# Zeroing the expert sum rows in the window attention stage instead of the projection stage

## The reference

```python
mod = silu(cond) @ w_ada + b_ada                 # 6 x 1024 columns, for c_ctx and for c
h = modulate(rms_norm(x), shift1, scale1)
q_g, k_g, v_g, g_g, lora, q_s, k_s, v_s = split(h @ w_in)
gla  = gated_linear_attention(q_g, k_g, v_g, lora) -> rms_norm -> * silu(g_g)
attn = sink_softmax(q_s @ k_s) @ v_s             # tile 0: 128 context keys;
                                                 # latents: cached context keys + own tile and its neighbours
x = x + g1 * (concat(gla, attn) @ w_out)
x = x + g2 * moe(modulate(rms_norm(x), shift2, scale2))   # 64 experts, 8 per token, 1 shared
return rms_norm(x), new keys and values, new states
```

## Time and profile before

| | |
|---|---|
| median of 3 runs | 1649.61 us (1646.57 to 1650.51) |
| the profiled execution | 1649.61 us, span 1647.8 us |
| PE busy | 1510.6 us, 92% of the span |
| mean granted clock of TensorE | 0.956 of full |
| PE in window_attention (439.8 to 600.4 us) | busy 153.17 of 160.6 us |
| DMA | 297.40 MB in the whole run |

### The profile page before, as it was taken

How to read it: one execution, slowest core, us unless ns; L and a number is a source line. 1 busy time by engine, 2 the same in 40 slices (tenths; PEclk the granted TensorE clock), 3 DMA queues, 4 the chain that set the end, 5 groups by cost and what they waited for, 6 DMA issues and landing times. The chain is left out here.

```text
span 1647.8 us, 29332 instructions
## 1 busy us (share of the span) xinstructions
PE 1510.6 (92%) x9399; PEld 942.9 (57%) x9400; DVE 725.9 (44%) x1468; ACT 530.2 (32%) x1255; POOL 563.8 (34%) x615
## 2 busy tenths in 40 slices
PE   5999999999799999999999599999899999999745
PEld 2654678788677785555455355555455555555312
DVE  2300143442555563688752244444344444444238
ACT  2400174442265631121100133333333333333212
POOL 0001134343343211111145345555445555445422
PEclk7899999999899999999999799999999999999868
DMA  9981001100383032002000599999999999986487
GB/s 338 352 326 39 19 19 38 43 14 17 108 304 108 2 138 104 39 26 116 1 0 0 203 301 335 334 331 340 346 338 332 339 291 314 257 227 118 64 300 299
DMA packets 107962, 297.40 MB, mean 180 GB/s; under 512 B 12830, under 2 KB 23922, under 8 KB 107634
## 3 DMA queue, kind: packets, MB, share of 16 engines
q1 hardware_dynamic: 80674, 207.83, 33.4%
q0 software_dynamic: 25920, 83.91, 21.3%
q10 hardware_dynamic: 1296, 4.72, 0.7%
HBM read 226.02 MB, written 80.87 MB: 186 GB/s over the span
## 5 line engine op out<-in xcount | busy, mean ns | idle before, releaser
L2080 PE MATMUL ps_g<-w_exp,mix 128*64 x1408 | 327.1, 386 | 5.7 <-DVE own_gu L2175 2.8
L2083 PE MATMUL ps_g<-own_gu,mix 128*64 128x256 f32 x1408 | 327.1, 386 | 0.0
L2080 PEld LDWEIGHTS ps_g<-w_exp,mix 128*64 128x64 f32 x1408 | 187.6, 138 | 108.3 <-issue 11.4
L2083 PEld LDWEIGHTS ps_g<-own_gu,mix 128*64 128x64 f32 x1408 | 187.6, 138 | 0.0
L2029 POOL DMA_INDIRECT sum_rows<-mix,scatter_row x66 | 127.8, 1936 | 173.2 <-DVE mix L2118 146.9
L2052 PE MATMUL ps_y<-w_exp,hidT 128*64 x352 | 171.6, 610 | 6.2 <-ACT own_d L2131 6.2
L2053 PE MATMUL ps_y<-own_d,hidT 128*64 128x512 f32 x352 | 171.6, 610 | 0.0
L511 PE MATMUL ps_f<-late,hT 128*128 128x256 f32 x624 | 143.0, 386 | 0.0
L2175 DVE COPY own_gu<-w_exp 128x2048 f32 x89 | 109.2, 1227 | 61.2 <-issue 44.9
L511 PEld LDWEIGHTS ps_f<-late,hT 128*128 128x128 f32 x624 | 118.6, 193 | 18.1 <-issue 1.9
L2002 POOL DMA_INDIRECT mix<-h_rows,gather_row x92 | 99.0, 1076 | 78.7 <-POOL gather_row L1999 53.1
(11 more groups left out here) (339 smaller groups left out, 2553.9 us busy)
## 6 DMA issues: line engine op xcount, KB each, us to landing
w_exp<-in_exp_w_gate SPq DMA_DIRECT2D x64, 512.0 KB
w_exp<-in_exp_w_up SPq DMA_DIRECT2D x64, 512.0 KB
w_exp<-in_exp_w_down SPq DMA_DIRECT2D x64, 512.0 KB
sum_rows<-mix SPq DMA_DIRECT2D x10, 2048.0 KB, 18.4
sums<-sum_rows SPq DMA_DIRECT2D x36, 512.0 KB
ada_ring<-in_w_ada SPq DMA_DIRECT2D x8, 2048.0 KB, 11.0
wring<-in_w_ada SPq DMA_DIRECT2D x3, 2048.0 KB, 13.1
h_rows<-h SPq DMA_DIRECT2D x9, 512.0 KB, 2.6
```

The source lines that it names most:

```text
L2080: pe.matmul(ps_g[par][0:HALF, 0:2 * FF].rearrange("p (k f) -> p k f", k=2), xT[par][:, j * P:j * P + HALF], w[:, bass.ds(slot * 3, 2), ff] ...
L2083: last = pe.matmul(ps_g[par][HALF:P, 0:2 * FF].rearrange("p (k f) -> p k f", k=2), xT[par][:, j * P + HALF:(j + 1) * P], own_gu[par][:, :, ...
```

## The change

The ten zeroing stores move from SP's queue in project to SP's queue in window_attention. There they read a new tile `zero_row`, 128x1024, which POOL sets to 0 before its first rope work. They are issued two behind each of the first two ada loads and one behind each of the other six. Each store still writes 2 MB, now in rows of 1024 elements where it was rows of 512. SP's wait for all ten is at the stage's end. Tile 0's mask is read from the new tile, and `no_mask` with its memset on DVE goes. `turn_k(0)` and `turn_k(1)` move ahead of the loop over `m` on PE, and ACT's `keep_k(1, 0)` and `keep_k(2, 1)` with them.

```diff
 project
-        zero = keep["mix"][:, (2 * NT - 1) * 512:]
-        zeroed, sums_zero = sem("zero_made"), sem("sums_zero")
-            sp.wait_ge(zeroed, 1)
-            for k in range(10):
-                rows = dram["y"][k % 2].rearrange("(p t) n -> p t n", p=P)[:, 4 * (k // 2):4 * (k // 2) + 4, :]
-                sp.dma_start(rows.rearrange("p t (h n) -> p (t h) n", n=512),
-                             zero.unsqueeze(1).to_broadcast([P, 8, 512])).then_inc(sums_zero, 16)
-            sp.wait_ge(sums_zero, 160)
-            pool.memset(zero, 0.0).then_inc(zeroed, 1)
 window_attention
-        no_mask = sb("no_mask", [P, P])
-        unmasked = sem("no_mask_made")
+        zero = sb("zero_row", [P, D])
+        zeroed, sums_zero = sem("zero_made"), sem("sums_zero")
                 sp.dma_start(ring[i % RING][:], ...).then_inc(ring_in[i % RING], 16)
+                if i == 0:
+                    sp.wait_ge(zeroed, 1)
+                for k in range(*((2 * i, 2 * i + 2) if i < 2 else (i + 2, i + 3))):
+                    rows = dram["y"][k % 2].rearrange("(p t) n -> p t n", p=P)[:, 4 * (k // 2):4 * (k // 2) + 4, :]
+                    sp.dma_start(rows, zero[:].unsqueeze(1).to_broadcast([P, 4, D])).then_inc(sums_zero, 16)
+            sp.wait_ge(sums_zero, 160)
+            pool.memset(zero[:], 0.0).then_inc(zeroed, 1)      # POOL, before the first rope
 PE
             turn_q(0)
+            turn_k(0)
+            turn_k(1)
             for m in range(N + 2):
-                if m < 2:
-                    turn_k(m)
 ACT
             keep_q(0)
+            keep_k(1, 0)
+            keep_k(2, 1)
             for m in range(N + 1):
-                    if m < 2:
-                        keep_k(m + 1, m)
 DVE
-            dve.memset(no_mask[:], 0.0).then_inc(unmasked, 1)
-                    dve.wait_ge(unmasked, 1)
+                    dve.wait_ge(zeroed, 1)
-                mask = bias[:, c:c + w] if t else no_mask[:]
+                mask = bias[:, c:c + w] if t else zero[:, 0:w]
```

## The result

The changed kernel takes 1657.88 us, median of 11 runs (1655.54 to 1660.43), against 1648.93 us for the kernel before in the same session (11 runs, 1646.57 to 1654.35). The ratio is 1.0052, interval 1.0042 to 1.0062: slower by 0.52%, or 8.6 us (6.9 to 10.2) by that ratio; the two medians are 8.95 us apart. The forecast was 1657.3 us. The profiled execution of the changed kernel took 1656.29 us with a span of 1654.5, so 6.7 us more than that of before, less than the medians differ.

What follows compares the result with a forecast made beforehand. PE sets the pace, and a transfer matters only where PE waits for it. A 5.8 us wait for load 2 plus 1.9 us of clock gave 7.7 us on 1649.6, so 1657.3 us; range 1649.8 to 1664.0.

Steps and rivals of the forecast that it cites:

- Project, 0 us: Project stage: taking out ten stores, a POOL memset and an SP wait changes 0 us, covered by PE's unbroken work.
- the 0.5 allowed: Sign in the changed profile: the window attention stage starts within 0.5 us of the kernel before.
- POOL memset, 0.9 us: Window attention's start: the memset ahead of the first rope delays the second rope and turn_k(2) by 0.9 us.
- Moved turns, 0: Window attention's start: scores(0) starts some 4.7 us later but fills PE's 3.99 us hole, costing nothing beyond the memset.
- Shift at item 1, 0.3 us: First ada item: its 0.59 us load wait swallows part of the memset's 0.9, leaving 0.3 us, bounds 0 to 1.0.
- Stores ahead of loads, 5.3 us each: SP's queue: each store ahead delays an ada load by 5.3 us; load 2 late by 5.8, load 3 by 7.1.
- The rival that the stores don't delay the loads: SP's queue: loads run beside or overtake stores, leaving only 0.3 to 0.9 us, 1649.9 to 1650.5; chance 0.19.
- Mixing slower: Rival, window attention: mixed loads and stores at 335 GB/s, 1663.9 us; chance 0.18, shared with a long low clock.
- Clock, 1.9 us: Second ada item: its wait halves PE's clock for 3.8 us, losing 1.9 us, bounds 0 to 5.7.
- the two bounds: Second and third ada items: 7.7 us by load 2's wait plus clock, 7.1 by load 3, which adds nothing.
- The clock comes back earlier: Rival, before the first ada item: full clock sooner, 2.7 us faster, 1646.9, only if loads are in time; chance 0.05.
- The sum, 7.7 us: Second ada item: 5.8 us wait for load 2 plus 1.9 us of lost clock, 7.7 us slower in all.

Runs made afterwards that it cites:

- the stores late: Changed kernel with all ten stores behind ada loads 4 to 8, two behind each, none behind the first three: 1649.59 us, ratio 0.9993 to before.
- The repetition: The changed kernel run once more, unaltered, beside the kernel with 40 identity products on PE: ratio 1.0056 to before.
- stores alone: Changed kernel with the turn_k moves undone and the zero tile set by DVE instead of POOL: 1658.10 us, ratio 1.0050 to before.
- the turns alone: Kernel before with only turn_k(0), turn_k(1) and ACT's two copies moved ahead of the loop: 1651.17 against 1649.93 us, ratio 1.0003.
- one store ahead: Changed kernel with one store ahead of each ada load from load 2 on, two behind each of the last two: ratio 1.0002 to before.
- three: Changed kernel with three stores ahead of ada load 2, three more ahead of load 3, one behind each of the last four: ratio 1.0108 to before.
- `turn_k(2)` later: Kernel before with only turn_k(2) and its copy on ACT moved behind scores(3): ratio 0.9997 to before.
- The run with 20 products: Changed kernel with 20 products of the identity with itself on PE ahead of the second ada item's wait: 1658.57 us, ratio 1.0041 to before.
- the first of the two runs: Changed kernel with 40 products of the identity with itself on PE ahead of the second ada item's wait: 1659.41 us, ratio 1.0057 to before.

## Why the prediction was right

**Project, 0 us.** Right. With the stores late, nothing is left of the change but the empty project stage and the start, and the time is 0.9993 of before. The profiles say it more directly: PE's first product of the linear attention stage starts at 201.45 to 201.86 us in the five kernels with the stores in project, and at 199.09 to 201.97 in the nine without. The means, 201.64 and 201.16, are closer together than the nine are among themselves. The window attention stage of the changed kernel did start 1.04 us later, more than the 0.5 allowed. That came from the linear attention stage, which began at 201.10 and took 1.80 us longer than before. Between 220 and 240 us the granted clock of this execution was 0.91 (second row), where it was 1.00 before (first row):

```profile
220.00:240.00 20.00, 17.23 (x146) 14.43 (x146) 9.12 (x18) 14.64 (x47) 13.18 (x20) 1.00 0.00 1
...
220.00:240.00 20.00, 17.20 (x138) 14.12 (x137) 9.81 (x20) 13.73 (x44) 12.46 (x19) 0.91 0.00 1
```

The repetition started the window attention stage at 437.12 and the kernel with stores alone at 439.71, so this is a difference between executions.

**POOL memset, 0.9 us.** It took 0.95. `turn_k(2)` at 452.39 is 11.55 us into the stage and was at 10.64: 0.91 later, as the prediction had it.

**Moved turns, 0.** Right in mechanism and size: the turns alone gave 1.0003. `scores(0)` started at 447.45, 6.61 us into the stage; the prediction's 446.5 was 6.7.

**Shift at item 1, 0.3 us.** 0.24 in the changed kernel and 0.43 in its repetition, but 0.84 with the stores late, 1.14 with one store ahead and 1.18 with three, over the prediction's upper bound of 1.0. It isn't the memset alone: with `turn_k(2)` later, a kernel without the memset, item 1 comes 1.25 us later than before. In all four it waits for load 1, whose landing scatters by about a microsecond.

**Stores ahead of loads, 5.3 us each.** Right, and a little high: 4.9 to 5.3 by the landings of load 2. The one tiny load that the trace of before had in line stood for big loads too. The rival that the stores don't delay the loads fell with one store ahead against three: 0 and then 8.27 us of wait, at the slack that the prediction gave. Item 2 came 5.0 and 5.3 us later than before, where 5.8 was reckoned; load 3 landed at 474.1 + 18.1 = 492.2, 51.4 us into the stage, 19.6 later than before, where 21.2 was reckoned, and PE, at item 3 at 52.36, didn't have to wait for it.

**Mixing slower.** It was not. The prediction feared 335 GB/s; the mixed traffic ran at 393 to 424 from 458 to 500, and no item waited for load 3 in the changed kernel.

**Clock, 1.9 us.** 1.4 to 2.4, from two executions of the changed kernel and one with the stores alone. What the sum didn't say is how near the two bounds stand: it found load 3 at 7.1 and the clock's path at 7.7, and took the larger. By its own terms the clock was worth only 0.6 us of time. The run with 20 products shows just that: item 3 is still 6.3 us late, by load 3.

**The clock comes back earlier.** In the profiled execution of the changed kernel it did: item 1 took 2.81 us, not 3.64, and PE reached item 2 at 469.03, 28.19 us into the stage instead of 29.15. It gained nothing, as the prediction's condition says: load 2 was late, and the wait of 5.99 took it in. In the repetition it did not come back earlier: item 1 took 3.64 us there.

**The sum, 7.7 us.** By profiles, the stage grew by 6.44 us in the changed kernel, by 7.65 in its repetition and by 7.68 with the stores alone. By the timed runs it is 8.6 us (6.9 to 10.2) and 1.0056 for the repetition. 7.7 lies inside. The two terms make up the whole of each profile's growth: 5.03 + 1.41 = 6.44, 5.28 + 2.37 = 7.65, 5.26 + 2.42 = 7.68. That the forecast came within 0.6 us of the measured median is in part luck: the base of 1649.6 us, the median of three runs, was 0.7 us above the 1648.93 of eleven, and the growth by the timed runs is 0.9 us more than forecast. Within the growth, the wait was set 0.5 to 0.8 us too high and the clock between 0.5 too high and 0.5 too low. Whether the microsecond between 7.7 and 8.6 is real stays open; nothing in the rest of the profile accounts for it. After the stage, the changed kernel needs 1044.52 us and the one before 1045.30.

Off was a detail: the DMA engines stayed full (share 1.04) not until about 505 but until 545, since from item 3 on they still work off stores. It cost nothing: load 4 landed at 502.7 (483.3 + 19.4), 9 us before its item.

## What to carry to other kernels

A transfer that nobody waits for isn't free when it is put ahead of one that somebody does: price it as its bytes at the queue's rate, add it to the landing of every load behind it, and compare with the slack of each. Here the slack of 4.9 us took one store of 5 us, and the same ten stores behind the last urgent load cost nothing that could be measured. Where several waits follow each other closely, look behind the one that you remove: moving `turn_k(2)` alone only made the wait for load 1 longer, and only both moves together gave a gain that the timed runs show, 0.3%.

## What was unexpected of the hardware

- Loads and stores mixed ran faster than this stage's loads alone: 393 to 424 GB/s from 458 to 500 us of the changed kernel, against 386 to 389 where the kernel before has loads alone in this stage (its windows, columns as above):

```profile
456.00:460.00 4.00, 4.00 (x24) 2.21 (x18) 0.29 (x1) 1.59 (x8) 0.00 (x0) 0.53 1.05 389
460.00:466.00 6.00, 5.70 (x49) 4.29 (x46) 3.80 (x15) 5.00 (x19) 3.46 (x3) 1.00 1.05 386
```

  Loads alone can be faster elsewhere: the load at 609 us ran at 434 GB/s. The stores are written here in rows of 4 KB; those in project, in rows of 2 KB, ran at 391. Whether the length of the rows or the mix makes the difference was not tested. The Trainium skill, DMA: Bandwidth & Descriptors, section Where 436 GB/s comes from, puts the memory side of one core at about 358 GB/s; these windows are all above it, and the measurement decides.
- A queue on another engine gave no relief at all: two stores on ACT's queue moved item 1, which waits for load 1, by 10.75 us, about as much as two stores in SP's own line.
- A 128x128 float32 product of the identity took 0.23 us (20 in 4.73, 40 in 9.20) back to back at full clock. That is twice what the first of the two runs was laid out for.
